# Pool mixer of a two-layer decoder trunk: VectorE's first tile ahead of the last maps' split, a weight unit split on GpSimd, token sums moved by a block and by a row

## What is computed

```python
for i in range(2):
    h = rmsnorm(x, norm_mix[i])
    if i == 0: x = x + conformer_conv_module(h, ...)
    else:      x = x + multiscale_pool_mixer(h, pool_w, pool_b, pool_scale)
    h = rmsnorm(x, norm_ffn[i])
    x = x + conv_ffn(h, ffn_w_up[i], ffn_w_dw[i], ffn_b_dw[i], ffn_w_down[i])
return rmsnorm(x, final_norm)

def multiscale_pool_mixer(h, w_grp, b_grp, scale):     # windows 2, 4, 8, 16, a group of 256 channels each
    pooled = trailing-window mean of h - h             # per group, fewer tokens at the start
    return scale * (einsum("bsgc,gce->bsge", pooled, w_grp) + b_grp)
def conv_ffn(h, w_up, w_dw, b_dw, w_down):             # FF = 2816
    up = h @ w_up; act, gate = up[..., :FF], up[..., FF:]
    return (silu(causal_dwconv(act, w_dw, b_dw)) * gate) @ w_down    # conv width 3
```

## Time and profile before

| | |
|---|---|
| median of 3 runs | 962.42 us (960.37 to 963.34) |
| the profiled execution | 960.57 us |
| its span, first to last instruction | 958.8 us |
| TensorE busy | 942.4 us (98%) |
| VectorE, ScalarE, GpSimd busy | 553.7, 387.0, 106.8 us |
| share of TensorE in the chain that ended last | 94% |
| granted TensorE clock, mean | 0.994 |
| maps, window sums, first FFN step of layer 1 | 559.6, 572.8, 583.7 us |

### The profile page before, as it was taken

The page is one execution under the profiler, slowest core; times in us unless marked ns, Lnnn a source line. Parts: engine busy times, 40 slices in busy tenths (PEclk is TensorE's granted clock), DMA queues, the critical chain, the costliest instruction groups (busy, mean ns, idle before and its releaser), DMA issues.

```text
span 958.8 us, 11895 instructions
## 1 busy us (share of the span) xinstructions
PE 942.4 (98%) x4510; PEld 792.5 (83%) x4510; DVE 553.7 (58%) x707; ACT 387.0 (40%) x592; POOL 106.8 (11%) x71
## 2 busy tenths in 40 slices
PE   7999999999999999999999999999999999999996
PEld 6889898888888888888888898788888888888886
DVE  6899895557555565564433359666555555532333
ACT  7785685444333333342322355433334333321220
POOL 0658795000000000000000000000000000000000
PEclk9999999999999999999999999999999999999998
DMA  7220022223322223312222332223222222223212
GB/s 266 100 88 1 1 92 85 89 88 95 124 88 87 87 87 99 119 60 90 91 90 96 112 109 89 86 92 119 97 87 87 87 92 99 67 90 114 90 61 89
DMA packets 17020, 88.56 MB, mean 92 GB/s; under 512 B 2016, under 2 KB 4320, under 8 KB 9952
## 3 DMA queue, kind: packets, MB, share of 16 engines
q1 hardware_dynamic: 16416, 87.67, 26.9%
q10 hardware_dynamic: 576, 0.52, 0.2%
HBM read 86.09 MB, written 2.10 MB: 92 GB/s over the span
## 4 chain that ended last, share of the span: by engine, by line
PE 94%; DVE 2%; DMA 1%; ACT 1%; issue 1%; SPq 1%; POOL 0%; DVEq 0%
PE bank L1062 29%; PE bank L1064 29%; PE bank L1063 29%; PE bank L1112 2%; PE bank L1113 2%; PE bank L1114 2%; DMA w_raw<-w_pw 1%; PE bank L1123 1%; DVE out_sb L1053 1%; DVE w_lo L728 1%; PE bank L1129 0%; PE bank L1247 0%; PE bank L1244 0%; PE bank L1243 0%; ACT w_hi L436 0%
## 5 line engine op out<-in xcount | busy, mean ns | idle before, releaser
L1062 PE MATMUL bank<-h_hi,w_hi 128*128 128x512 f32 x816 | 318.8, 391 | 2.2 <-DVE w_lo L728 1.3
L1064 PE MATMUL bank<-h_hi,w_lo 128*128 128x512 f32 x816 | 317.5, 389 | 0.0
L1063 PE MATMUL bank<-h_lo,w_hi 128*128 128x512 f32 x816 | 317.5, 389 | 0.0
L436 ACT ACTIVATE w_hi<-w_raw 128x2048 fp32r<-128x2048 f32 (+2 forms) x88 | 149.2, 1695 | 212.9 <-PE bank L1064 212.8
L728 DVE TENSOR_TENSOR w_lo<-w_raw,w_hi 128x2048 fp32r<-128x2048 f32 (+2 forms) x82 | 164.4, 2005 | 101.5 <-ACT w_hi L436 100.7
L1062 PEld LDWEIGHTS bank<-h_hi,w_hi 128*128 128x128 f32 x816 | 153.2, 188 | 35.0 <-issue 1.8
L1063 PEld LDWEIGHTS bank<-h_lo,w_hi 128*128 128x128 f32 x816 | 153.2, 188 | 32.1 <-issue 0.5
L1064 PEld LDWEIGHTS bank<-h_hi,w_lo 128*128 128x128 f32 x816 | 153.2, 188 | 31.9
L1063 PE MATMUL bank<-u_lo,w_hi 128*128 128x512 f32 (+1 forms) x422 | 159.5, 378 | 0.0
L1062 PE MATMUL bank<-u_hi,w_hi 128*128 128x512 f32 (+1 forms) x374 | 141.1, 377 | 0.4 <-DVE w_lo L728 0.4
L1064 PE MATMUL bank<-u_hi,w_lo 128*128 128x512 f32 (+1 forms) x374 | 140.8, 376 | 0.0
(11 more groups left out here) (183 smaller groups left out, 927.3 us busy)
## 6 DMA issues: line engine op xcount, KB each, us to landing
w_raw<-w_up SPq DMA_DIRECT2D x44, 1024.0 KB, 4.9
w_raw<-w_down SPq DMA_DIRECT2D x32, 704.0 KB, 4.0
w_raw<-w_pw SPq DMA_DIRECT2D x11, 1024.0 KB, 4.8
x_res<-x SPq DMA_DIRECT2D x3, 512.0 KB, 7.5
out<-out_sb SPq DMA_DIRECT2D x12, 128.0 KB, 1.8
w_raw<-w_pw SPq DMA_DIRECT2D x4, 256.0 KB, 7.2
w_raw<-w_pool SPq DMA_DIRECT2D x2, 512.0 KB, 3.6
band_raw<-band SPq DMA_DIRECT2D x1, 800.0 KB, 5.4
```

Of the source, the lines that this page charges most:

```text
L436: nc.scalar.activation(w_hi[s][:, 0:columns], w_raw[s][:, 0:columns], ACT.Copy).then_inc(w_rounded[s], 1)
L1062: M.matmul(dst, a, hi, start=start, stop=False)
L1063: M.matmul(dst, a, lo, start=False, stop=False)
L1064: return M.matmul(dst, b, hi, start=False, stop=stop)
```

## The change

Four moves, no arithmetic is different.

1. GpSimd splits unit 0 of the FFN's first step (`split(0, M_UP[1])`, its last instruction); VectorE's `split_unit` of it goes.
2. VectorE updates tile 0 ahead of the splits of group 3's maps. Behind them its order is: update 1, split 0, update 2, split 1, updates 3 and 4, split 2, update 5, split 3, update 6, split 4, update 7, splits 5 to 7.
3. The token sums of the first norm stand behind block 0 of group 1 and not behind group 0.
4. In unit 1 of the first FFN step the token sums stand ahead of row 4 (before: 5), the spread ahead of row 6 (before: 7).

```diff
@@ gpsimd
                 nc.gpsimd.tensor_tensor(v_lo[:, c, :], conv_out[:, c, :], as_f32(v_hi[:, c, :]), SUB).then_inc(v_split, 1)
+            split(0, M_UP[1])
@@ vector
-                    for group in range(len(WINDOWS)):
-                        if group == 3:
-                            split_unit(0, M_UP[1], UNIT)
+                    def split_maps(group):
                         for j in range(BLOCKS):
...
-                    dve.wait_ge(shifted, KD)
-                    for c in range(KD):
+                    def update(c):
...
-                        if c:
-                            split_updated(c - 1)
-                    split_updated(KD - 1)
+                    for group in range(3):
+                        split_maps(group)
+                    dve.wait_ge(shifted, KD)
+                    update(0)
+                    split_maps(3)
+                    update(1)
+                    split_updated(0)
+                    update(2)
+                    split_updated(1)
+                    update(3)
+                    update(4)
+                    split_updated(2)
+                    update(5)
+                    split_updated(3)
+                    update(6)
+                    split_updated(4)
+                    update(7)
+                    for c in range(5, KD):
+                        split_updated(c)
@@ tensor, second_norm
-                if k == 5:
+                if k == 4:
                     pe.wait_ge(summed, (KD + 1) * 4)
...
-                if k == 7:
+                if k == 6:
                     spread(1)
@@ tensor, maps
                             last.then_inc(map_mm, 1)
-                        if group == 0:
-                            pe.wait_ge(summed, (KD + 1) * 3)
-                            sum_by_token(sumsq[:, :], start=True, stop=True).then_inc(stat_mm, 1)
+                            if (group, j) == (1, 0):
+                                pe.wait_ge(summed, (KD + 1) * 3)
+                                sum_by_token(sumsq[:, :], start=True, stop=True).then_inc(stat_mm, 1)
```

## The result

The changed kernel is a little slower: median 963.6 us of 11 runs (961.05 to 965.56) against 961.77 for before beside it (11 runs, 960.21 to 963.34), ratio 1.0022, 95% interval 1.0014 to 1.003, so +2.1 us (+1.3 to +2.9). The forecast was 959.7; the second rival (TensorE waits for tile 0, and its clock falls in the hole) gave 964.3. The profiled execution took 961.68 us.

What follows compares the result with a forecast made beforehand. TensorE was taken to bound the kernel, busy 942.4 of 958.8 us, so only its holes could be won. 1.62 (FFN start) + 1.08 (loop entry) = 2.70 off the median 962.42 gave 959.7 us, range 958.5 to 965.3.

Steps and rivals of the forecast that it cites:

- lower end of its bounds: Tile 0's update beside GpSimd's split: `L1016` takes the 0.22 us it takes alone; chosen with much doubt.
- `L816` rows: Earlier trace rows: VectorE's `L816`, one SBUF and one PSUM input, takes 748 ns beside a GpSimd split, 749 over the program.
- upper end: Tile 0's update: `L1016` waits for the rest of GpSimd's split, from 573.55 to 576.68, 3.13 us more.
- The Trainium skill's rule: VectorE instructions with two SBUF inputs and GpSimd instructions reading SBUF exclude each other; first issued holds the shared port throughout.
- Rival 1: Window sums: GpSimd's split holds tile 0, updates come 3.13 us later, FFN at 585.22; net +0.43, 962.9 us; chance 0.32.
- rival 2: Window sums: tile 0 held and TensorE's clock falls in the hole, losing 1.5 us; +1.9, 964.3 us; chance 0.20.
- Token sums behind another block: First norm: six group-1 matmuls ahead of the token sums fill 0.72 of a 0.74 us hole; sums still start at 563.16.
- VectorE's timetable: Pool mixer: VectorE's steps from tile 0 at 573.36, GpSimd's split 572.05 to 576.68, FFN at 582.09.
- the 1.62: FFN start: 582.09 instead of 583.71, 1.62 us won, including 0.72 from the first norm's token sums.
- Row change: First FFN step: token sums and spread one row earlier remove the whole 1.08 us loop-entry hole, with 0.9 in hand.
- rival 3: First FFN step: VectorE's sum of squares over 0.9 us late, so the row change gains nothing; -1.6, 960.8 us; chance 0.06.
- 3.39 us of holes: TensorE's waits at token sums, window sums and loop entry, 559 to 610 us; the most any edit there can bring.

Runs made afterwards that it cites:

- E1: Changed kernel with tile 0's partial sum in a PSUM bank, so `L1016` reads one SBUF and one PSUM tensor: 958.43 us, ratio to before 0.9964.
- E5: Changed kernel with three GpSimd memsets of `w_lo` in place of its weight split, low part left out of the product: one execution, 959.87 us.
- E3: Changed kernel with eleven idle constant products on TensorE ahead of tile 6's window sums, in the hole: 962.21 us, ratio to before 1.0003.
- E9: Changed kernel with token sums and spread back in their old places, leaving VectorE's order and GpSimd's split: 965.56 us, ratio to before 1.0041.
- E2: Kernel before with only the token-sum and spread moves; VectorE and GpSimd as they were: 958.68 us, ratio to before 0.9967.
- E8: Kernel before with tiles 6 and 7 in banks 2 and 3, first norm's token sums and the spread moved, no GpSimd split: 958.11 us, ratio 0.9972.
- E7: Changed kernel with tile 0's partial sum in PSUM and window sums of tiles 6 and 7 in banks 2 and 3: 958.37 us, ratio to before 0.997.
- E10: Changed kernel, partial sum still in SBUF, with window sums of tiles 6 and 7 in banks 2 and 3: 960.66 us, ratio to before 0.9985.
- E4: Changed kernel with GpSimd's weight split in eight instructions of 256 columns instead of one of 2048: 959.36 us, ratio to before 0.9975.

## Why the prediction was wrong, and where it was right

**The step that failed** is the choice for tile 0's `L1016` beside GpSimd: the sum took the lower end of its bounds, 0.22, "nearest to the `L816` rows", and the upper end, 3.13 more, came true: 3.09 instead of 0.22, which is 2.87 more, since the instruction's own 0.22 lies within the wait. The earlier trace rows was no evidence: it showed an instruction with one SBUF input and one in PSUM, and E1 shows that just this makes the difference. The Trainium skill's rule ("SBUF — State Buffer", section "Who interferes with whom"), which the prediction quoted and weighed too low, agrees with every run here: held to the end of the GpSimd instruction that was first (3.09, 2.10, 0.62, 0.40), not held with a PSUM input (E1) nor beside GpSimd that only writes (E5). The other order, VectorE first and GpSimd waiting, occurs in no run. The `L816` rows lacked the feature in dispute, a second SBUF input, so they gave no reason to go against the rule.

**The rivals.** Rival 1's timetable held: tile 5 at 577.88 (forecast 577.9), tile 6 at 582.07 (582.28), tile 7 at 583.84 (584.05), 0.21 early because the 3.13 counted the instruction's own 0.22 as well. The FFN came at 585.97, not at 585.22, since rival 2's clock fell as well: 1.50 by trace where the prediction said 1.5, and +1.7 in sum where it said +1.9. E3 shows that this part is the clock: with matmuls in the hole it is gone. The objection put against it, that two tiles of window sums stand in the hole, was no help: they run behind the 3.12, not within it. That the 1.5 was met so well is in part luck, since E9 has the same hole and a cost of 2.86.

**Token sums behind another block: right.** The sums start at 563.15 (forecast 563.16) without a wait, E2 has the 0.72 alone.

**VectorE's timetable: right but for that one instruction.** It began tile 0 at 573.41 (forecast 573.36), GpSimd's split ran 572.09 to 576.69 (572.05 to 576.68), and TensorE never waited for that unit. But the 1.62 were to come with tile 1's `L1016` at 576.23 by the forecast's own steps (576.04 and an instruction), which also lies ahead of 576.68; the prediction named only split 0 as in reach. E1 shows this second meeting, 0.40. Without any hold F - S would be 19.01 (E5), 1.54 below before, with it 19.22: the forecast said 20.55 - 1.62 = 18.93. So but for the hold the sum of 2.70 was nearly right (2.6 in E5's trace, 2.4 in E1's).

**Row change: right.** No hole at the loop entry in any run with the sums ahead of row 4. E2 has the token moves alone; E9 lacks them and has the hole. In E8, with the sums still ahead of row 5, the spread's move alone left no hole either. The sum of squares was ready 0.8 ahead of the sums in E1 (598.94 against 599.78; the forecast had 0.9 in hand), and where the FFN starts earliest or VectorE is latest, in E7 and E10, TensorE lost at most 0.2 on it; rival 3 did not come.

**What wasn't asked.** Of the 3.39 us of holes listed, the 1.57 at the window sums were taken for VectorE's to give. They came from reuse of two banks, while two others lay free: E7 and E8 remove them whole, though E8 by its trace loses 0.87 again behind the FFN's start.

## What to carry to other kernels

Before work is moved to GpSimd, go through VectorE's list for the length of the GpSimd instruction and count the tensors that each instruction reads from SBUF. With two, it waited here to the end of the GpSimd instruction that read SBUF, although it was one column wide, and everything behind it in order waited too. A PSUM operand (E1) or GpSimd's work in pieces (E4) avoids or shortens that. If such a delay opens a hole of about 3 us in TensorE, price the clock as well (1.5 and 2.9 us in the two traces here that show it), and ask first whether the wait can be removed by another bank instead of by a faster engine; then look at what waits next (0.87 in E8).

## What the runs showed of the hardware beyond that

The same kernel's runs scatter by some 3 us, and the profiles show where a good part of it may come from. In layer 0, about 148 to 156 us, behind one-column matmuls (`L1123`), TensorE is at 1.2 GHz for a time that differs from run to run, with the same instructions ahead. Two windows of E3, where the low clock begins early and ends late:

```profile
148.00:150.00 2.00, 2.00 (x12) 2.00 (x12) 0.00 (x0) 0.44 (x1) 0.00 (x0) 0.51 0.49 119
...
154.00:156.00 2.00, 2.00 (x16) 2.00 (x16) 1.89 (x4) 0.37 (x2) 0.00 (x0) 0.78 0.03 8
```

and the same of E7:

```profile
148.00:150.00 2.00, 2.00 (x16) 1.62 (x15) 0.33 (x2) 0.18 (x2) 0.00 (x0) 1.00 0.99 287
...
154.00:156.00 2.00, 2.00 (x15) 1.66 (x13) 2.00 (x4) 1.94 (x4) 1.05 (x1) 1.00 0.03 8
```

S, the start of the token sums 400 us later, lies at 562.77 in E7, 563.15 in the changed kernel, 565.49 in E3 and 565.72 in E10: 2.95 us between executions of untouched code. The low clock is not all of it: E7 and E2 have the same granted clock there (1.00 over 144 to 150 us, 0.72 over 150 to 156), and S at 562.77 and 563.82. That is why S is subtracted above. What decides how long the low clock lasts there stays open; no run here was made for it. It bears on every single execution, and perhaps on E2's surplus, since medians of five runs can fall on one side of such a scatter; that too is argued, not shown.
